# mLSTM heads on one NeuronCore: roots, normalisations and gates moved behind the last step, and the low parts of four weight rows made on GpSimd

## The reference, cut to what matters

```python
def mlstm_readout(hf, hb, act, z, norm_w, skip):
    h = hf + hb                                    # both directions of a head
    mu = jnp.mean(h, axis=-1, keepdims=True)
    var = jnp.mean(jnp.square(h - mu), axis=-1, keepdims=True)
    hn = (h - mu) * lax.rsqrt(var + EPS)
    ...
    return (hn * norm_w + skip * act) * silu(z)

m = mlstm_readout(hf_l, hb_l, act_l, z_l, lp['mlstm_norm_w'], lp['mlstm_skip'])   # 512 wide
f = fourier_mix(u_l, lp['w_fourier'])                                             # 512 wide
y = jnp.concatenate([m, f], axis=-1) @ lp['w_out']                                # 1024 x 1024
```

## Time and profile before

| what | value |
|---|---|
| median of 3 runs | 1861.33 us (1857.40 to 1863.47) |
| the profiled execution's own time | 1863.57 us |
| its span, first to last instruction | 1861.4 us |
| TensorE matmuls busy | 1774.4 us, 95% of the span |
| VectorE busy | 1228.1 us, 66% |
| ScalarE busy | 920.0 us, 49% |
| GpSimd busy | 150.5 us, 8% |
| mean granted TensorE clock | 0.97 of full speed |
| chain of work that ended last | TensorE 87%, VectorE 7%, ScalarE 4%, DMA 1% |

### The profile page before, as it was taken

How to read it: one execution, slowest core, us unless ns; L and a number is a source line. 1 busy time by engine, 2 the same in 40 slices (tenths; PEclk the granted TensorE clock), 3 DMA queues, 4 the chain that set the end, 5 groups by cost and what they waited for, 6 DMA issues and landing times.

```text
span 1861.4 us, 25489 instructions
## 1 busy us (share of the span) xinstructions
PE 1774.4 (95%) x9041; PEld 1464.3 (79%) x9041; DVE 1228.1 (66%) x2205; ACT 920.0 (49%) x1499; POOL 150.5 (8%) x170
## 2 busy tenths in 40 slices
PE   7899999999999998999999999999979889999997
PEld 6777788888887876888888888886667778888885
DVE  5565878887225648478866333755564679898988
ACT  4447632232214548452323213533563568888885
POOL 1000200000000100021100000400000111111002
PEclk9999999999999999999999999899989789999999
DMA  6323335445332124326644432410310389999994
GB/s 179 89 70 132 91 99 140 136 137 146 114 101 81 47 93 156 104 78 192 187 142 139 120 94 87 123 46 1 103 57 27 130 300 395 392 377 378 374 379 178
DMA packets 203854, 289.31 MB, mean 155 GB/s; under 512 B 12332, under 2 KB 150548, under 8 KB 203636
## 3 DMA queue, kind: packets, MB, share of 16 engines
q1 hardware_dynamic: 189060, 240.60, 38.8%
q0 software_dynamic: 11920, 36.48, 6.3%
q10 hardware_dynamic: 2784, 11.01, 1.5%
HBM read 271.77 MB, written 21.53 MB: 158 GB/s over the span
## 4 chain that ended last, share of the span: by engine, by line
PE 87%; DVE 7%; ACT 4%; DMA 1%; issue 1%; SPq 0%; DVEq 0%; POOL 0%; ACTq 0%; POOLq 0%
PE bank L200 24%; PE bank L202 23%; PE bank L201 23%; PE bank L69 11%; PE bank L899 2%; DVE weights_low L226 1%; PE bank L2707 1%; ACT weights_high L220 1%; DVE tmp L69 1%; DVE conv_x L69 1%; DMA ring<-in_w_out 1%; PE bank L3056 1%; PE bank L327 1%; DVE ring L69 1%; DVE z_and_u L69 1%
## 5 line engine op out<-in xcount | busy, mean ns | idle before, releaser
L226 DVE TENSOR_TENSOR weights_low<-ring,weights_high 128x1024 fp32r<-128x1024 f32 x180 | 219.7, 1224 | 319.5 <-ACT weights_high L220 319.0
L200 PE MATMUL bank<-XH,weights_high 128*128 128x512 f32 x960 | 383.9, 400 | 15.2 <-DVE weights_low L226 9.3
L202 PE MATMUL bank<-XH,weights_low 128*128 128x512 f32 x960 | 376.4, 392 | 0.0
L201 PE MATMUL bank<-XL,weights_high 128*128 128x512 f32 x960 | 375.9, 392 | 0.0
L220 ACT CAST weights_high<-ring 128x1024 fp32r<-128x1024 f32 x180 | 187.9, 1048 | 371.5 <-PE bank L202 366.9
L200 PEld LDWEIGHTS bank<-XH,weights_high 128*128 128x128 f32 x960 | 181.5, 189 | 59.0 <-issue 10.2
L202 PEld LDWEIGHTS bank<-XH,weights_low 128*128 128x128 f32 x960 | 181.4, 189 | 39.1
L201 PEld LDWEIGHTS bank<-XL,weights_high 128*128 128x128 f32 x960 | 181.9, 189 | 35.8 <-issue 0.5
L2747 DVE TENSOR_TENSOR XL<-ring,XH 128x1024 fp32r<-128x1024 f32 x144 | 169.8, 1219 | 10.9 <-ACT XH L2741 10.9
L2741 ACT CAST XH<-ring 128x1024 fp32r<-128x1024 f32 x144 | 145.2, 1049 | 0.5 <-PE bank L202 0.3
L69 DVE SCALAR_TENSOR_TENSOR squares<-ring,c_silu,squares 128x128 f32<-128x128 f32 x384 | 135.1, 352 | 13.6
(11 more groups left out here) (607 smaller groups left out, 3463.8 us busy)
## 6 DMA issues: line engine op xcount, KB each, us to landing
ring<-in_w_ffn_in SPq DMA_DIRECT2D x88, 512.0 KB, 4.8
ring<-in_w_gate SPq DMA_DIRECT2D x72, 512.0 KB, 5.5
ring<-in_w_up SPq DMA_DIRECT2D x72, 512.0 KB, 7.4
ring<-in_w_down SPq DMA_DIRECT2D x72, 512.0 KB, 5.4
ring<-in_w_ada POOLq DMA_DIRECT2D x48, 512.0 KB, 4.6
ring<-in_w_ffn_out SPq DMA_DIRECT2D x44, 512.0 KB, 3.5
ring<-in_w_out SPq DMA_DIRECT2D x20, 512.0 KB, 3.5
slot_output<-expert_out SPq DMA_DIRECT2D x18, 512.0 KB, 6.7
```

The costliest lines, as they stand in the source:

```text
L200: PE.matmul(out_ap, w_h, x_h, start=first, stop=False, skip_group_check=True)
L201: PE.matmul(out_ap, w_h, x_l, start=False, stop=False, skip_group_check=True)
L202: return PE.matmul(out_ap, w_l, x_h, start=False, stop=last, skip_group_check=True)
L226: eng.tensor_tensor(wl[:, s, :], ring[s][:, :], wh[:, s, :].bitcast(F32), ALU.subtract).then_inc(split_done.sem, 1)
```

## The change

The call `skip_and_gate` is split in three: `gate_turn` (skip on ScalarE, turns on TensorE), `gate` (two VectorE passes and the cast on ScalarE) and `gate_low` (the subtraction on VectorE). `center` for heads 0 and 1 stays in steps 3 and 5; every `normalize_head` and every gate stands after step 8 now. `root_table` moves from step 8 to step 7. Rows 4 and 5 of `w_out` are cast in steps 2 and 3 (before: 5 and 6), rows 6 and 7 in steps 6 and 7 (before: both in 7), and all four subtractions are on GpSimd. The groups of chunks 0 and 2 and the shift rows move within steps 6 to 8, and the groups of chunks 6, 7, 1, 4 and 5 are laid between the gates. Nothing of the arithmetic changes.

```diff
--- before.py
+++ after.py
@@ -2453,19 +2453,28 @@
                 normalized[h] = vec.do(V.tensor_scalar, hs[h][:, cols], hs[h][:, cols], mean[:, ch:ch + 1],
                                        inv[:, ch:ch + 1], ALU.add, ALU.mult)
 
-        def skip_and_gate(h, b=5):
-
-            skipped = act.do(S.activation, ac[:, h, TM:], ac[:, h, TM:], ACT.Copy, scale=column["m_skip"][:, h:h + 1],
-                             after=[scored[h], ktok_done[h]])
+        turned, skipped, gate_high = {}, {}, {}
+
+        def gate_turn(h, b=5):
+
+            skipped[h] = act.do(S.activation, ac[:, h, TM:], ac[:, h, TM:], ACT.Copy, scale=column["m_skip"][:, h:h + 1],
+                                after=[scored[h], ktok_done[h]])
             pe.need(normalized[h], *bank_free[b])
             for ch in range(TT):
                 cols = slice(ch * P, (ch + 1) * P)
-                t = pe.do(PE.transpose, bank[b][:, cols], hs[h][:, cols], ident)
+                turned[h] = pe.do(PE.transpose, bank[b][:, cols], hs[h][:, cols], ident)
+
+        def gate(h, b=5):
+
             t = vec.do(V.scalar_tensor_tensor, hs[h], bank[b][:, :], column["m_norm"][:, h:h + 1], ac[:, h, TM:],
-                       ALU.mult, ALU.add, after=[t, skipped])
+                       ALU.mult, ALU.add, after=[turned[h], skipped[h]])
             bank_free[b] = [t]
             t = vec.do(V.tensor_tensor, hs[h], hs[h], zu[:, h, :], ALU.mult, after=[t, z_done])
-            gated[h] = split_to(XH[:, h, :], XL[:, h, :], hs[h], [t])
+            gate_high[h] = act.do(S.copy, XH[:, h, :], hs[h], after=[t])
+
+        def gate_low(h):
+
+            gated[h] = vec.do(V.tensor_tensor, XL[:, h, :], hs[h], XH[:, h, :].bitcast(F32), ALU.subtract, after=[gate_high[h]])
 
         load(pool, lr, wrt[:, :, 0:4], I["w_router_group_2"][0].rearrange("(k p) n -> p k n", p=P))
         load(pool, lr, wrt[:, :, 4:20], I["w_router_expert_2"][0].rearrange("(k p) n -> p k n", p=P))
@@ -2488,9 +2497,9 @@
 
             if row < 6:
                 S.wait_ge(used_done.sem, slot_used[row - 4])
-            t = act.do(S.copy, out_high[row], out_raw[:, row % 2, :], after=[l_out[row % 2].now()])
-            out_split[row] = vec.do(V.tensor_tensor, out_low[row], out_raw[:, row % 2, :], out_high[row].bitcast(F32),
-                                    ALU.subtract, after=[t])
+            t = act.do(S.copy, out_high[row], out_raw[:, row % 2, :], after=[l_out[row % 2].now(), *([k_done[MH - 1]] if row > 5 else [])])
+            out_split[row] = pool.do(G.tensor_tensor, out_low[row], out_raw[:, row % 2, :], out_high[row].bitcast(F32),
+                                     ALU.subtract, after=[t])
 
         def out_begin(row, *chunks):
 
@@ -2536,31 +2545,37 @@
         for part in range(4):
             tokens_of(0, part, b=(5, 0, 1, 2)[part])
         scores(0)
-        for n in range(2 * MH + 3):
+        for n in range(2 * MH + 2):
             h, d = n // 2, n % 2
             ahead = n < 2 * MH - 2
             if n < 2 * MH:
                 weighted_keys(n)
             if 1 <= n <= 2 * MH:
                 weighted_scores(n - 1)
-            if 2 <= n < 2 * MH + 2:
+            if n == 2 * MH:
+                out_begin(6, 0, 2)
+            if n >= 2:
                 outputs(n - 2)
             if 1 <= n <= 2 * MH:
                 key_products(n - 1)
-            if n == 2 * MH:
-                shift_half(0)
-                out_begin(6, 0, 2)
-                out_begin(7, 0, 2)
-                shift_half(1)
-                for row in range(4, 8):
-                    out_begin(row, 3)
             if n < 2 * MH:
                 exponents(n)
                 if n and d == 0:
                     scores(h)
                 if n + 3 < 2 * MH:
                     row_load(n + 3)
-            if 2 <= n < 2 * MH + 2:
+            if n == 6:
+                for c in (0, 2):
+                    out_begin(4, c)
+                    out_begin(5, c)
+            if n == 7:
+                shift_half(0)
+            if n == 2 * MH:
+                out_begin(7, 0, 2)
+                shift_half(1)
+                for row in range(4, 8):
+                    out_begin(row, 3)
+            if n >= 2:
                 divisors(n - 2)
                 combine(n - 2)
             if ahead:
@@ -2568,39 +2583,46 @@
                 tokens_of(h + 1, 2 * d + 1, b=0)
             if 1 <= n <= 2 * MH:
                 states(n - 1)
-            if n == 2 * MH:
-                root_table()
-            if n >= 3 and d and (n - 3) // 2 < MH:
+            if n in (3, 5):
                 center((n - 3) // 2)
-            if n >= 4 and n % 2 == 0 and n // 2 - 2 < MH:
-                normalize_head(n // 2 - 2)
             if ahead:
                 features(h + 1, d)
-            if n >= 5 and d and (n - 5) // 2 < MH:
-                skip_and_gate((n - 5) // 2, b=2 if n == 5 else 5)
-            if n == 5:
-                out_weights(4)
-            if n == 6:
-                out_weights(5)
-                out_begin(4, 0)
-                out_begin(5, 0)
+            if n in (2, 3):
+                out_weights(n + 2)
+                out_load(n + 4, out_split[n + 2])
+            if n in (6, 7):
+                out_weights(n)
             if n == 7:
-                for row in (6, 7):
-                    out_load(row, out_split[4], out_split[5])
-                    out_weights(row)
-                out_begin(4, 2)
-                out_begin(5, 2)
                 sp.need(row_read[2 * MH - 1], row_read[2 * MH - 3])
                 for s in range(2):
                     load_half(out_src, 0, s)
+                root_table()
             if n == 2 * MH:
                 router_consts = router_constants()
-            if n == 2 * MH + 1:
-                for row in range(4, 8):
-                    out_begin(row, 6, 7)
+                center(2)
+                normalize_head(0)
+                normalize_head(1)
+        gate_turn(0)
+        gate(0)
+        center(3)
         for row in range(4, 8):
-            out_begin(row, 1, 4)
-        skip_and_gate(MH - 1)
+            out_begin(row, 6, 7)
+        gate_turn(1)
+        gate_low(0)
+        gate(1)
+        normalize_head(2)
+        gate_low(1)
+        for row in range(4, 8):
+            out_begin(row, 1)
+        gate_turn(2)
+        gate(2)
+        normalize_head(3)
+        gate_low(2)
+        for row in range(4, 8):
+            out_begin(row, 4)
+        gate_turn(3)
+        gate(3)
+        gate_low(3)
         for row in range(4, 8):
             last = out_begin(row, 5)
             if row < 6:
```

## The result

The changed kernel takes 1851.13 us (median of 19 runs, 1846.68 to 1855.75), the kernel before 1861.33 us in the same comparison (19 runs, 1857.40 to 1866.60). The ratio is 0.9944, with a 95% interval from 0.9933 to 0.9955. The forecast was 1851. Of all the runs behind this text one, of the kernel with the rows' part alone, took 2541.37 us at a mean granted clock of 0.64 where its others have 0.97 or more, and it is left out of that kernel's median and ratio.

What follows compares the result with a forecast made beforehand. TensorE was taken as the bound, busy 95% of the span, with idle time and a low clock in the mLSTM stage to win back. 12.0 us less 1.5 for the clock, 10.5, led from median 1861.33 to 1851; range 1844 to 1860.

Steps and rivals of the forecast that it cites:

- The sum: From step 3 of the mLSTM loop to `stream`: the new order is 12.0 us shorter, before any clock loss.
- GpSimd against VectorE: Low-part subtractions: a VectorE instruction with two SBUF inputs that meets one is held up to 2.55 us.
- The clock: TensorE, loop and end: idle holes may lower its clock; about one loss, 1.5 us, bounds 0 and 13.
- five holes: TensorE idle times of 2.1, 2.1, 1.8, 2.2 and 1.1 us in the new order, each in dense work.
- Roots, gates, tables: Loop steps: four table loads (5.2 us of ScalarE), a 2.85 us VectorE wait, normalising and gates leave.
- A sign that failed: VectorE in the loop: weighted scores of steps 5 and 6 were to come about 5 us earlier.
- A: Rival, loop: GpSimd hinders nobody and the clock holds; 16.3 us gained, so 1845; chance 20%.
- B: Rival, end gates: two or three clock losses and more GpSimd meetings spend the gain; 1856 to 1859; 20%.
- C: Rival, TensorE from 1380.25: clock falls and stays down until `stream` runs; 9.7 us slower, 1871; chance 6%.
- D: Rival, loop: ScalarE becomes the last engine, so the loop gains nothing; 1855 to 1861; chance 4%.
- the ring: Each loop step: `outputs` needs the states, VectorE needs the outputs and makes the next states behind its queue.
- The anchor: Whole kernel: profiled execution 1863.6 less 10.5 gives 1853.1; it lay 2.2 above the median, hence 1850.8.

Runs made afterwards that it cites:

- the rows' part alone: Kernel before, with only the casts of rows 4 to 7 in steps 2, 3, 6, 7 and subtractions on GpSimd; 1857.41 us, ratio 0.9984.
- the repeat: The changed kernel run again with one register operation more per engine; 1851.20 us, ratio 0.9949 to the kernel before.
- the hole was filled: Changed kernel plus 24 small matmuls whose result nobody reads, on TensorE before the `outputs` of step 4; 1846.84 us in one run.
- the late subtractions: Changed kernel, with GpSimd's subtractions of rows 4 and 5 issued behind the divisors of the next step; 1847.52 us, ratio 0.9936.
- The parts alone: Besides the rows' part alone, the gates' part: changed kernel with rows cast and subtracted as before, on VectorE; 1852.95 us, ratio 0.9956.

## Why the prediction was right, point by point

**The sum.** The stage was forecast 12.0 us shorter, less 1.5 for the clock: 10.5. It is 10.9 shorter, and 10.4 in the repeat. Its points in time, with 4.28 added to those of after:

| TensorE reaches | before | forecast | after |
|---|---|---|---|
| `outputs` of step 4 | 1349.63 | 1352.0 | 1351.67 |
| `outputs` of step 5 | 1355.75 | 1360.1 | 1360.44 |
| `outputs` of step 6 | 1364.90 | 1366.35 | 1367.01 |
| `outputs` of step 8 | | 1380.25 | 1380.72 |
| first turn | | 1394.3 | 1394.89 |
| third turn | | 1405.8 | 1406.32 |
| fourth turn | | 1410.2 | 1411.18 |
| `stream` | 1427.12 | 1415.1 | 1416.21 |

The forecast column is without any clock loss. The kernel after is 0.3 us ahead of it at the first point, behind by 0.3 to 0.7 from the second to the sixth, and by 1.1 at the end: the two jumps are the two places where the clock fell. The idle times before step 6, step 8, the first and the third turn were forecast as 1.15, 2.1, 1.8 and 2.2 and are 1.20, 1.72, 1.73 and 1.97; those before step 5 (2.1) and the fourth turn (1.1) are 0.90 and none, since TensorE at the low clock was busy into them. So the walk along the queues, in start-to-start times of one trace, held to 1.1 us over the 71 us from its start at 1343.84.

**GpSimd against VectorE.** Right in kind and nearly in size: 2.74 us where "near 3 us" stood, and its end tied to GpSimd's. The subtraction took 2.36 us, not 2.55: doubling the 128x512 of the earlier trace rows added 1.05 to 1.31. In step 4 the prediction had the small passes of the divisors held; in the trace it is weighted q, which waits 1.12 us for TensorE, slow at that moment, and starts 0.21 us behind GpSimd. Where the hole was filled and the clock kept, weighted q was through in time and the divisors were held, as forecast. The price is about the same whichever it is (2.0 or 2.2 us), since both are in one queue. In step 7 a hold of 0.6 was paid where 1.2 was forecast. Without the three holds the sum should have been 4.3 us better; the late subtractions took away two of them and gave 3.8, of which some 1.1 is the clock that the held step had cost.

The Trainium skill ("SBUF — State Buffer", section "SBUF: two separate sides") says that the shared pair of ports goes to whichever comes first, for its whole instruction, against VectorE instructions with two SBUF inputs. The traces agree, in both directions: six passes shown here were held (2.74, 2.69, 1.30, and 2.73, 2.06 and 2.33 in the experiments), and those with a PSUM input (1.50 for four, 0.69) weren't, and the subtraction of GpSimd's that began while a VectorE pass that had been held was running took 2.68 us in place of 2.36.

**The clock.** The total was nearly right, the places were not, and here the prediction has its one real gap. It listed five holes and priced one loss at 1.5 us. It left out the hole before the `outputs` of step 4, though it was in reach: the work ahead of them is done at 1349.63 - 1.21 = 1348.42 before, nothing in the new order touches it, and the `outputs` were forecast for 1352.0, which makes a hole of 3.6. In after it is done at the same point (1347.39 - 3.25 + 4.28 = 1348.42), the hole came (3.25 us), and in every trace that has it the clock fell. Filling it gave 1.07 us back; the second loss, behind 1.97 us, cost 0.35. Together 1.4 in after, over two losses and not one, and some 1.9 in the repeat, where the second cost 0.87. A loss was priced at up to 2.6 us, of which idle time would pay half; the ones measured cost 0.35 to 1.07. So that 1.5 came out is in part luck: a missing hole and a price too high made up for each other. The clock over the middle window is 1.00 (0.98 over the times as the prediction wrote them, 1364.9 to 1404), where above 0.9 was asked.

**Roots, gates, tables.** Four table loads, the wait of 2.85 us on the first root and the holes of 3.81 and 2.42 us are gone. The parts alone put 6.5 of the stage's gain to the gates' side and 3.1 to the rows'. That the router's copies hold squares and roots back was forecast, and the experiment that puts the copies behind gains 2.3 us: it was on the path.

**A sign that failed.** The weighted scores of steps 5 and 6 were to come "about 5 us earlier". Step 6's started at 1372.21 and come at 1363.90 + 4.28 = 1368.18: 4.0 earlier. Step 5's started at 1359.23 and come at 1356.02 + 4.28 = 1360.3, not earlier at all, which the prediction's own `outputs(3)` at 1360.1 against 1355.75 before would have told: until step 5 the new order is the slower one.

**The rivals.** A (GpSimd hinders nobody) is refuted by the holds; its 16.3 us off the stage are what the late subtractions come near, with 14.7. B (the gain spent in the end) happened by 0.35 us of the 5 it needed. C (the clock falls in the end and stays down) didn't: it held behind 1380, and where it fell, at 1402.27, it was back at 1405.69. D (ScalarE the last of the ring) isn't seen in after, where each hole shown is ended by VectorE. It shows where something else is moved: VectorE waits for ScalarE's casts when the subtractions are its own, and with the late subtractions the `outputs` of step 5 wait 0.84 us for ScalarE.

**The anchor.** The profiled execution of before was 2.2 us over its median, and that of after is 3.4 under. Of the 5.7 us between the two, 4.3 lie upstream of the change. In the twelve traces of before, after and the experiments TensorE has the same hole of 1.8 us near 1230. In five of them the 24 matmuls behind it take 2.89 us and the loop's first `outputs` start at 1332.8 to 1334.1; in seven they take 3.84 to 4.34 and the `outputs` start at 1335.5 to 1339.3. Of the ten kernels with a median of several runs, the five that kept the clock there lie 1.2 to 3.4 us under theirs, the other five 0.2 under to 4.6 over. Taking the gain from the profile's own time and then carrying it to the median was what kept this out of the forecast. What makes one execution lose the clock there and another keep it stays open.

## What to carry to other kernels

Before a subtraction goes to GpSimd, look at what VectorE does in that time: beside passes that read PSUM it is free, beside a pass with two SBUF inputs it stops the whole VectorE queue until GpSimd's end, however small that pass is; a wait that places it behind the last such pass gained 3.8 us of the stage here. When you walk a new order through, list every hole that it makes, those in the part that gets slower too, before you price the clock. And compare two traces from the last point that the change can't have touched: 4.3 of the 15.2 us between these two profiles were never the change's.

## What the runs showed of the hardware

- A VectorE pass with two SBUF inputs that meets a GpSimd subtraction ends a fixed time behind it: 0.54 to 0.56 us for a 512-wide one (the three in after and that of the earlier trace rows), 0.02 to 0.03 for one of 4 elements (three cases). So it starts its own work only when GpSimd is done. With two of GpSimd's subtractions back to back, a VectorE pass of 512 elements that waited for the first still ran before the second was over (it ended at 1350.04, GpSimd at 1352.25), and the second subtraction took 2.68 us in place of 2.36.
- GpSimd's subtraction took 1.31 us for 128x512 and 2.36 us for 128x1024; VectorE's of 128x1024 takes 1.23.
- The same idle time doesn't always cost the clock. In otherwise dense work, 3.25 to 5.13 us did in all seven traces that have it, single ones of 1.20 to 1.21 in none (thirteen cases), and single ones of 1.70 to 1.80 in this stage in none either (sixteen cases), while behind 1.8 us near 1230 it fell in seven of twelve. Behind 1.97 us it fell within 0.6 us in two traces, 1.3 us later in one, and held in four; in two of these it fell 6.5 and 6.7 us on, behind holes of 1.0 and 0.84.
